# Modulation with eight and two column groups in one accumulator each, summed at the seams, and a gate's row sums by fp32r products

## The chip, the cores and the metric

One NeuronCore of a Trainium2 chip runs the whole kernel. The metric is the device time of one execution in microseconds. The kernel before takes 2351.67 us (median of three runs, 2350.42 to 2352.06).

## The reference, cut to what matters

Two transformer blocks of width 2048 over 256 tokens. The second block is modulated: a vector `c` of 2048 numbers goes through SiLU and through a weight matrix of 2048 by 12288, and the result, cut in six, shifts, scales and gates the two halves of the block:

```
c_act = jax.nn.silu(c)
mod = (c_act @ w_ada[l] + b_ada[l])[:, None, :]
sh1, sc1, g1, sh2, sc2, g2 = jnp.split(mod, 6, axis=-1)
h = rms_norm(x, norm_mix[l]) * (1.0 + sc1) + sh1
x = x + g1 * hybrid_mixer(h, ...)
h = rms_norm(x, norm_ffn[l]) * (1.0 + sc2) + sh2
x = x + g2 * conv_glu_ffn(h, ...)
```

All the rest (first block with attention, gated linear attention and a gated FFN; second block's mixer and FFN with a convolution) is unchanged by the change.

## The kernel before, in words

The kernel runs six stages one after the other: `FirstMixer`, `Glu`, `Down` (first FFN), `SecondMixer`, `ConvGlu`, `Down` again. Every large product is made in three fp32r products of high and low parts. Weights arrive from HBM over SP's DMA queue: `load` (L245 on) brings 1 MiB as two transfers of 512 KiB into a ring of four (`raw_weights`), ScalarE copies the high part (`split_hi`, L289), VectorE subtracts the low part (`split_lo`, L297), and TensorE multiplies (L330, L608, L1858, L2216). A unit is half a load; ScalarE and VectorE are three units ahead of TensorE. SP issues in program order, and each load waits until the ring's slot has been split.

The modulation (`c_act @ w_ada`, 96 MiB of weights) isn't done on TensorE. Its 12288 columns are cut in twelve groups of 1024 columns. `Ada.load` (L488 on) brings 256 rows of one group as one transfer of 1 MiB (128 partitions of two rows, 4 KiB each) into one of two buffers (`ada_w`); it waits until the products of the load before the last are done. `Ada.product` (L501 on) multiplies one of the two rows of each partition by its `c` on VectorE and adds it to an accumulator `ada_acc` of 128 partitions by 1024: sixteen steps a group, the first of which is a plain multiply (L518), the others multiply and add (L516). Then each group's accumulator has to be summed over its 128 partitions. The groups and what sums them:

- group 0: products in the last ticks of `FirstMixer`; groups 1 to 5: products in `Glu`, two turns each. Each of these six is summed in `Glu`: `turned` makes eight TensorE transposes (L460) and `reduced` one VectorE reduction of 128x1024 out of PSUM (L467).
- groups 6, 7, 8: products in `Down` (24 loads between k = 5 and the tail), each in an accumulator of its own. Groups 6 and 7 are summed at the start of `SecondMixer` with products by a column of ones (L1953, two instructions for each of the eight, since fp32 takes two), the last six of the second group's eight between `turn_early` (L2152) and the four `turn` (L2141) that the stage's first products wait for.
- group 8 goes to HBM and back, and group 9 (products in `SecondMixer`) too; both are summed at the start of `ConvGlu` (L3616 by ones, L460 by transposes), with the last columns' scales made inside the first turn (`last_scales`).
- groups 10 and 11, the second gate, are needed along the rows: `row_sums` (L3646) multiplies ones by the accumulator, in fp32, in two places of `ConvGlu`.

Of the kernel before, what the change touches and what calls it, by code (L numbers as in the profile page):

```python
# [21 lines left out]
ds = bass.ds  # L22
# [38 lines left out]

COLS = {}
_n = 0
for _name, _w in (("attn_norm_w", 16), ("ffn_norm_w", 16), ("norm_mix_2", 16), ("norm_ffn_2", 16), ("c_2", 16),
# [3 lines left out]
                  ("conv_w0", 88), ("conv_w1", 88), ("conv_w2", 88), ("conv_b", 88), ("b_ada_2", 96)):  # L68
# [13 lines left out]
def constants():  # L82
# [4 lines left out]
    parts = [("ident", r == c), ("ones", np.ones((P, P))), ("headsum", same),  # L87
             ("incl", same & (r <= c)), ("anti", same & (r >= c))]
# [33 lines left out]
class Kit:  # L122


    def __init__(self, nc, ctx, ins, at):
# [28 lines left out]
        self.ada_w = [self.sem("ada_w0"), self.sem("ada_w1")]  # L154
# [302 lines left out]
def turn_sums(kit, acc, bank):  # L457

    for q in range(8):
        step = kit.nc.tensor.transpose(kit.ps[:, bank + q // 4, (q % 4) * P:(q % 4 + 1) * P], acc[:, q * P:(q + 1) * P],  # L460
                                       kit.c("ident"))
    return step


def reduce_sums(kit, a, bank):

    return kit.nc.vector.tensor_reduce(kit.modcols[:, ds(a, 8)], kit.ps[:, bank:bank + 2, :].rearrange(  # L467
        "p b (q n) -> p (b q) n", n=P), AX, ALU.add)


def add_bias(kit, a, count):

    b = COLS["b_ada_2"] + a
    cols = kit.modcols[:, a:a + count]
    kit.dve(kit.nc.vector.tensor_tensor(cols, cols, kit.col[:, b:b + count], ALU.add))


class Ada:

    def __init__(self, kit, w, acc, free=None, stored=None):


        self.kit, self.w, self.acc, self.free, self.stored = kit, w, acc, free, stored

    def load(self, sp, lead, j, m):  # L488

        kit = self.kit  # L490
        if self.free:
            sp.wait_ge(*self.free)
            self.free = None
        a = 8 * lead + m
        if a >= 2:
            sp.wait_ge(kit.ada_acc, 2 * (a - 1) + 16 * j)
        w = kit.ins["w_ada_2"][0]
# [3 lines left out]
    def product(self, dve, lead, j, s, acc=None):  # L501
# [3 lines left out]
        if s == 0 and self.stored:  # L505
            dve.wait_ge(kit.ada_sum, lead - 1)
# [14 lines left out]
    def sums(self, pe, lead, j, bank=6):  # L521
# [3 lines left out]
        if lead > 1:  # L525
            pe.wait_ge(kit.ada_out, lead - 1 + j)
# [3409 lines left out]
```

## Time and profile before

| | |
|---|---|
| median of three runs | 2351.67 us |
| the profiled execution | 2352.51 us |
| its span, first to last instruction | 2350.7 us |
| granted clock of TensorE, mean | 0.997 |
| TensorE busy | 2337.8 us (99%) |
| TensorE weight loads busy | 2151.6 us (92%) |
| VectorE busy | 1616.4 us (69%) |
| ScalarE busy | 1153.2 us (49%) |
| SP's DMA queue, packets' time as a share of 16 engines | 68.3% |

"Busy" is the time in which at least one instruction of the engine was under way. [...] The share of a DMA queue is a mean over the 16 DMA engines; it says nothing on how the load is spread over them.

### The profile page before, as it was taken

What the parts mean: (1) busy time and instruction counts of PE and PEld (TensorE: products, weight loads), DVE (VectorE), ACT (ScalarE), POOL (GpSimd) and SP (SyncE); (2) the same over time, 40 slices, a digit from 0 to 9 for tenths busy, and PEclk for the clock granted to TensorE, in tenths of its full rate; (3) what the DMA queues carried; (4) which work ended last, traced back from release to release, by engine and by line L of the source; (5) the groups of instructions that cost most, each with busy time, mean ns of one, the idle gap of its engine ahead of it and who ended that gap; (6) DMA issues with size and microseconds to landing.
All of it is one profiled execution on the core that took longest, in us unless ns stands there. A gap on an engine that the chain in (4) does not pass through costs nothing.

```text
span 2350.7 us, 43754 instructions
## 1 busy us (share of the span) xinstructions
PE 2337.8 (99%) x17937; PEld 2151.6 (92%) x17937; DVE 1616.4 (69%) x1931; ACT 1153.2 (49%) x1510; POOL 5.1 (0%) x7
## 2 busy tenths in 40 slices
PE   9999999999999999999999999999999999999998
PEld 8889778999999999888999899888999999998887
DVE  5668568777777766877778455667878666665556
ACT  5565454534344344444764444546544445454444
POOL 0000000000000000000000000000000000000000
PEclk9999999999999999999999999999999999999999
DMA  8556567888888877898577545555778656665563
GB/s 308 167 179 197 159 234 271 278 282 297 282 282 295 282 242 263 316 324 315 175 279 269 163 130 153 196 200 187 283 255 295 208 179 206 196 206 197 192 192 117
DMA packets 233049, 543.62 MB, mean 231 GB/s; under 512 B 15610, under 2 KB 22596, under 8 KB 232260
## 3 DMA queue, kind: packets, MB, share of 16 engines
q1 hardware_dynamic: 232756, 540.97, 68.3%
q8 instruction: 110, 1.80, 0.3%
q10 hardware_dynamic: 144, 0.52, 0.1%
q14 instruction: 39, 0.32, 0.0%
HBM read 535.11 MB, written 6.32 MB: 230 GB/s over the span
## 4 chain that ended last, share of the span: by engine, by line
PE 98%; DVE 0%; ACT 0%; issue 0%; DMA 0%; SPq 0%; DVEq 0%; ACTq 0%
PE ps L330 37%; PE ps L1858 18%; PE ps L608 18%; PE ps L2216 16%; PE ps L1875 2%; PE ps L2509 0%; PE ps L1041 0%; PE ps L1053 0%; PE ps L1071 0%; PE ps L1083 0%; PE ps L2141 0%; PE ps L460 0%; PE ps L2744 0%; PE ps L1134 0%; PE ps L2921 0%
## 5 line engine op out<-in xcount | busy, mean ns | idle before, releaser
L297 DVE TENSOR_TENSOR weights_lo<-raw_weights,weights_hi 128x1024 fp32r<-128x1024 f32 x786 | 957.6, 1224 | 659.8 <-ACT weights_hi L289 658.0
L289 ACT ACTIVATE weights_hi<-raw_weights 128x1024 fp32r<-128x1024 f32 x782 | 827.2, 1062 | 1086.8 <-PE ps L330 446.4
L516 DVE SCALAR_TENSOR_TENSOR ada_acc<-ada_w,col,ada_acc 128x1024 f32<-128x1024 f32 x180 | 230.2, 1279 | 0.1
L330 PE MATMUL ps<-conv_x_hi,weights_hi 128*128 128x256 f32 x1280 | 198.0, 277 | 0.0
L330 PE MATMUL ps<-glu_x_hi,weights_hi 128*128 128x256 f32 x1280 | 197.7, 276 | 0.0
L330 PE MATMUL ps<-glu_x_hi,weights_lo 128*128 128x256 f32 x1280 | 197.2, 276 | 0.0
L330 PE MATMUL ps<-glu_x_lo,weights_hi 128*128 128x256 f32 x1280 | 197.2, 276 | 0.0
L330 PE MATMUL ps<-conv_x_lo,weights_hi 128*128 128x256 f32 x1280 | 197.2, 276 | 0.0
L330 PE MATMUL ps<-conv_x_hi,weights_lo 128*128 128x256 f32 x1280 | 197.2, 276 | 0.0
L330 PEld LDWEIGHTS ps<-conv_x_hi,weights_hi 128*128 128x128 f32 x1280 | 169.1, 188 | 1.0 <-issue 1.0
L330 PEld LDWEIGHTS ps<-glu_x_hi,weights_hi 128*128 128x128 f32 x1280 | 169.0, 188 | 0.0
L330 PEld LDWEIGHTS ps<-glu_x_lo,weights_hi 128*128 128x128 f32 x1280 | 168.9, 188 | 0.0
L330 PEld LDWEIGHTS ps<-glu_x_hi,weights_lo 128*128 128x128 f32 x1280 | 168.9, 188 | 0.0
L330 PEld LDWEIGHTS ps<-conv_x_hi,weights_lo 128*128 128x128 f32 x1280 | 168.9, 188 | 0.0
L330 PEld LDWEIGHTS ps<-conv_x_lo,weights_hi 128*128 128x128 f32 x1280 | 168.9, 188 | 0.0
L2216 PE MATMUL ps<-m_x_hi,weights_hi 128*128 128x256 f32 (+1 forms) x576 | 94.9, 288 | 0.1
L3800 DVE SCALAR_TENSOR_TENSOR conv_y<-ps,conv_taps,conv_y 128x255 f32<-128x255 f32 (+1 forms) x176 | 72.7, 476 | 29.8 <-ACT conv_y L3732 28.8
L2216 PE MATMUL ps<-m_x_lo,weights_hi 128*128 128x256 f32 (+1 forms) x576 | 89.8, 279 | 0.0
L2216 PE MATMUL ps<-m_x_hi,weights_lo 128*128 128x256 f32 (+1 forms) x576 | 89.2, 277 | 0.5 <-issue 0.5
L1858 PE MATMUL ps<-weights_hi,down_hi 128*128 128x512 f32 x288 | 89.0, 390 | 0.5 <-DVE stat L3804 0.2
L1858 PE MATMUL ps<-weights_hi,down_lo 128*128 128x512 f32 x288 | 88.7, 389 | 0.0
L1858 PE MATMUL ps<-weights_lo,down_hi 128*128 128x512 f32 x288 | 88.7, 389 | 0.0
(560 smaller groups left out, 3635.3 us busy)
## 6 DMA issues: line engine op xcount, KB each, us to landing
raw_weights<-in_w_in_dram SPq DMA_DIRECT2D x202, 512.0 KB, 5.0
ada_w<-in_w_ada_dram SPq DMA_DIRECT2D x96, 1024.0 KB, 6.1
raw_weights<-in_w_ffn_up_dram SPq DMA_DIRECT2D x176, 512.0 KB, 4.6
raw_weights<-in_w_gate_dram SPq DMA_DIRECT2D x88, 512.0 KB, 4.6
raw_weights<-in_w_up_dram SPq DMA_DIRECT2D x88, 512.0 KB, 4.6
raw_weights<-in_w_down_dram SPq DMA_DIRECT2D x88, 512.0 KB, 5.7
raw_weights<-in_w_ffn_down_dram SPq DMA_DIRECT2D x88, 512.0 KB, 4.3
raw_weights<-in_w_out_dram SPq DMA_DIRECT2D x64, 512.0 KB, 5.1
```

Of the source, the lines that this page charges most:

```text
L289: kit.nc.scalar.activation(kit.slots(n, i)[0], raw, ACT.Copy).then_inc(kit.w_hi, 1)
L297: kit.nc.vector.tensor_tensor(lo, raw, hi.bitcast(F32), ALU.subtract).then_inc(kit.w_lo, 1)
L330: ins = nc.tensor.matmul(out, lhsT=lhsT, rhs=rhs, start=start and m == 0, stop=(k == KT - 1 and m == 2), skip_group_check=True)
L516: step = nc.vector.scalar_tensor_tensor(acc, w, c, acc, ALU.mult, ALU.add)
L608: ins = nc.tensor.matmul(out, lhsT=lhsT, rhs=rhs, start=start and m == 0, stop=ends and m == 2, skip_group_check=True)
L1858: ins = nc.tensor.matmul(kit.ps[:, 4 * t + 2 * half + q, :], lhsT=lhsT, rhs=rhs, start=(k == 0 and m == 0), stop=ends and m == 2, skip_gro ...
L1875: ins = nc.tensor.matmul(kit.ps[:, 4 * t + 2 * half + q, :], lhsT=lhsT, rhs=w[:, q * UN:(q + 1) * UN], start=False, stop=k == w_tiles - 1 ...
L2216: ins = nc.tensor.matmul(out, lhsT=lhsT, rhs=rhs, start=start and m == 0, stop=ends and m == 2, skip_group_check=True)
L3800: nc.vector.scalar_tensor_tensor(y[:, j, q, b:S], self.tile(j, q)[:, 0:S - b], taps[:, j, tap, q:q + 1], y[:, j, q, b:S], ALU.mult, ALU.ad ...
```

## The change

The partition dimension of the accumulators is cut up. For the first eight groups (columns 0 to 8191) the 128 partitions hold eight groups of sixteen rows: step `s` takes sixteen rows of the matrix, and partition 16 g + r holds row r of group g. After 128 such steps one accumulator holds the eight groups, sixteen partitions each, and eight products with a mask of 128 by 8 (`oct`) sum all of them at the start of `SecondMixer`. Groups 8 and 9 are held in one accumulator in the same way, two groups of 64 rows (mask `half`, 32 steps), and are summed at the start of `ConvGlu`. Groups 10 and 11 are loaded as before. The number of steps (192) and of bytes stays. The sums of `Glu` (transposes and reductions) go; the accumulator is carried over from stage to stage (`prior`), only the second pair's goes through HBM, once. `c` is needed in two more layouts (`c_half`, `c_oct`), the latter by one more pack, its transpose and a small copy each two turns of `Glu`. Each load is now two transfers of 512 KiB, whose source is `(g n)` columns taken as `g r n`. The gate's accumulator is split in a high part (ScalarE) and a low part (VectorE), and its row sums are four fp32r products in place of two fp32 ones.

```diff
 class Ada:
+    def source(self, lead, j, s):
+
+        w = self.kit.ins["w_ada_2"][0]
+        if lead < 8:
+            rows = w[ds(OCT * (16 * lead + s) + 16 * OCT * j, OCT), 0:16 * UN]
+        elif lead < 10:
+            rows = w[HALF * (16 * (lead - 8) + s):HALF * (16 * (lead - 8) + s + 1), 16 * UN:20 * UN]
+        else:
+            rows = w[P * s:P * (s + 1), 2 * UN * lead:2 * UN * (lead + 1)]
+        return rows.rearrange("r (g n) -> g r n", n=2 * UN)
 
     def load(self, sp, lead, j, m):
...
-        sp.dma_start(self.w[:, m % 2, :, :], w[2 * m * P:2 * (m + 1) * P, ds(2 * UN * lead + 2 * UN * j, 2 * UN)]
-                     .rearrange("(k p) n -> p k n", p=P)).then_inc(kit.ada_w[m % 2], 16)
+        for s in (2 * m, 2 * m + 1):
+            sp.dma_start(self.w[:, m % 2, s % 2, :], self.source(lead, j, s)).then_inc(kit.ada_w[m % 2], 16)
...
+    def sums(self, pe, bank, mask, acc):
+
+        kit, (a, b) = self.kit, self.kit.at[mask]
+        n = b - a
         for q in range(8):
-            step = nc.tensor.matmul(kit.ps[:, bank, q:q + 1], lhsT=self.acc[:, q * P:(q + 1) * P],
-                                    rhs=kit.c("ones")[:, 0:1], start=True, stop=True)
+            step = kit.nc.tensor.matmul(kit.ps[:, bank, n * q:n * (q + 1)], lhsT=acc[:, q * P:(q + 1) * P],
+                                        rhs=kit.c(mask), start=True, stop=True)
         step.then_inc(kit.ada_sum, 1)
...
+    def summed(self, lead, bank, mask):
+
+        kit, (a, b) = self.kit, self.kit.at[mask]
+        n, first, bias = b - a, 8 * lead, COLS["b_ada_2"] + 8 * lead
+        cols, add = (x.rearrange("p (g q) -> p q g", q=8) for x in (kit.modcols[:, first:first + 8 * n],
+                                                                    kit.col[:, bias:bias + 8 * n]))
+        return kit.nc.vector.tensor_tensor(cols, kit.ps[:, bank, 0:8 * n].rearrange("p (q g) -> p q g", g=n), add, ALU.add)
...
 class Glu:
...
-            mid = (lambda: self.ada.turned(pe, self.lead, j)) if summed else None
...
-                if summed and s == begun:
-                    self.ada.reduced(dve, self.lead, j)
                 if half is not None and s % 2 == begun:
-                    self.ada.product(dve, self.lead, j, 8 * half + s // 2)
+                    q = 8 * half + s // 2
+                    if q == 0:
+                        a = COLS["c_oct"] + 16 * self.lead
+                        dve.wait_ge(kit.ada_acc, 16 * self.lead + 16 * j)
+                        nc.vector.tensor_copy(self.c_turn[:, :], kit.col[:, ds(a + 16 * j, 16)]).then_inc(self.s_c, 1)
+                        dve.wait_ge(self.s_c, 1 + j)
+                    self.ada.product(dve, self.lead, j, q, c=self.c_turn[:, q:q + 1])
...
 class SecondMixer:
...
     def tensor(self, pe):
         kit, nc = self.kit, self.kit.nc
         pe.wait_ge(self.squares_in, 8)
-        self.down.ada_sums(pe, 0)
-        self.down.ada_sums(pe, 1, 0, 2)
+        self.down.ada_sums(pe)
         pe.wait_ge(self.squares_in, 11)
         for k in range(4):
             self.turned.turn_early(pe, k)
-        self.down.ada_sums(pe, 1, 2, 8)
         for k in range(4):
             self.turned.turn(pe, k)
...
 class ConvGlu:
...
+    def scales(self, dve):
+
+        dve.wait_ge(self.kit.ada_sum, 2)
+        self.kit.dve(self.ada.summed(8, 1, "half"))
+
+    def row_sums(self, pe, g):
+
+        kit, nc = self.kit, self.kit.nc
+        pe.wait_ge(self.s_acclo, g + 1)
+        for b in range(2):
+            for acc in (self.acc_hi, self.acc_lo):
+                step = nc.tensor.matmul(kit.ps[:, 4 + 2 * g + b, :], lhsT=self.ones[:, :], rhs=acc[:, b * UN:(b + 1) * UN],
+                                        start=acc is self.acc_hi, stop=acc is self.acc_lo)
         step.then_inc(kit.ada_sum, 1)
```

## Rows read from the trace of the kernel before

**Rows 1.** The page: busy time of the engines; the chain that ended last, by engine.

```profile
PE 2337.8 (99%) x17937; PEld 2151.6 (92%) x17937; DVE 1616.4 (69%) x1931; ACT 1153.2 (49%) x1510; POOL 5.1 (0%) x7
...
PE 98%; DVE 0%; ACT 0%; issue 0%; DMA 0%; SPq 0%; DVEq 0%; ACTq 0%
```

**Rows 2.** Timeline of Glu's last sum (start, us, engine, line, operation, count).

```profile
866.08 1.04 PE L460 MATMUL ps<-cst,ada_acc 128*128 128x128 f32 x8
...
866.87 0.72 PE L330 MATMUL ps<-glu_x_hi,weights_hi 128*128 128x256 f32 x4
867.21 1.22 DVE L467 TENSOR_REDUCE modcols<-ps 128x8 f32<-128x1024 f32 x1
```

**Rows 3.** Timeline of the second gate's first row sums, and of 512-column products.

```profile
1131.26 0.62 PE L1875 MATMUL ps<-down_last_hi,glu_x_hi 128*128 128x512 f32 x2
...
1131.72 0.61 PE L1875 MATMUL ps<-down_last_lo,glu_x_hi 128*128 128x512 f32 x2
...
1731.30 0.62 PE L330 MATMUL ps<-conv_x_hi,weights_lo 128*128 128x256 f32 x4
...
1731.75 1.88 PE L3646 MATMUL ps<-ada_acc,cst 128*128 128x512 f32 x4
...
1733.94 0.64 PE L330 MATMUL ps<-conv_x_lo,weights_hi 128*128 128x256 f32 x4
```

**Rows 4.** Timeline of the start of the second mixer.

```profile
1150.20 2.25 PE L1953 MATMUL ps<-cst,ada_acc 128*128 128x1 f32 x12
...
1150.21 0.17 DVE L3547 SCALAR_TENSOR_TENSOR modT<-modcols,col 128x16 f32<-128x16 f32 x1
...
1150.44 0.71 ACT L2117 ACTIVATE m_scaled<-x_weighted,stat 128x512 f32<-128x512 f32 x1
...
1152.32 1.09 PE L2141 MATMUL ps<-cst,m_scaled 128*128 128x128 f32 x4
```

**Rows 5.** Windows (us; busy of each engine; PEclk, DMA share, GB/s): the two seams.

```profile
1151.00:1152.00 1.00, 1.00 (x6) 1.00 (x6) 0.84 (x3) 0.14 (x1) 0.00 (x0) 0.50 1.24 256
...
1158.00:1160.00 2.00, 2.00 (x20) 2.00 (x19) 1.21 (x3) 1.46 (x4) 0.00 (x0) 1.00 0.78 207
...
1616.00:1617.00 1.00, 0.67 (x6) 0.46 (x6) 0.57 (x2) 1.00 (x3) 0.00 (x0) 1.00 0.99 389
```

**Rows 6.** Windows: the four stretches in which modulation weights of groups 0 to 9 arrive.

```profile
325.70:421.00 95.30, 95.14 (x439) 78.43 (x439) 74.59 (x82) 50.08 (x70) 0.00 (x0) 1.00 0.86 309
...
478.30:856.00 377.70, 377.70 (x3334) 377.70 (x3333) 280.75 (x236) 154.95 (x147) 0.00 (x0) 1.00 0.83 288
...
913.00:1110.00 197.00, 197.00 (x871) 163.13 (x870) 153.40 (x155) 87.58 (x109) 0.00 (x0) 1.00 0.89 321
...
1191.00:1265.00 74.00, 74.00 (x611) 72.08 (x610) 62.57 (x71) 41.41 (x56) 0.00 (x0) 1.00 0.85 313
```

**Rows 7.** DMA view of 320 to 420 us: GB/s in forty slices of 2.5 us.

```profile
GB/s 0 202 283 415 403 395 404 388 386 388 392 375 401 189 209 367 374 292 41 293 336 406 209 180 374 370 316 98 376 329 61 0 167 401 406 385 370 191 355 411
```

**Rows 8.** Timeline of SP: modulation loads in Glu, in Down, and first and last in the second mixer.

```profile
481.78 0.48 SPq L498 DMA_DIRECT2D ada_w<-in_w_ada_dram  x1
...
492.66 0.47 SPq L498 DMA_DIRECT2D ada_w<-in_w_ada_dram  x1
...
1004.50 0.38 SPq L498 DMA_DIRECT2D ada_w<-in_w_ada_dram  x1
...
1012.66 0.38 SPq L498 DMA_DIRECT2D ada_w<-in_w_ada_dram  x1
...
1191.11 0.37 SPq L498 DMA_DIRECT2D ada_w<-in_w_ada_dram  x1
...
1256.26 0.37 SPq L498 DMA_DIRECT2D ada_w<-in_w_ada_dram  x1
```

**Rows 9.** Timeline of SP: issues of vectors of 16 rows and of 4 rows.

```profile
16.17 0.42 SPq L829 DMA_DIRECT2D pack<-in_c_dram  x1
...
17.39 0.29 SPq L829 DMA_DIRECT2D pack<-in_rwkv_w_dram  x1
```

More of the change, by code:

```diff
@@ L503, in product, with scalar @@
+    def scalar(self, lead, s):
+        name, first = ("c_oct", 0) if lead < 8 else ("c_half", 8) if lead < 10 else ("c_2", lead)
+        return self.kit.cols(name, 16 * (lead - first) + s)
+    def product(self, dve, lead, j, s, acc=None, prior=None, c=None):
         nc, kit = self.kit.nc, self.kit
         m, k = s // 2, s % 2
-        if s == 0 and self.stored:
-            dve.wait_ge(kit.ada_sum, lead - 1)
-            dve.wait_ge(self.stored, 16)
-        elif s == 0 and lead and acc is None:
-            dve.wait_ge(kit.ada_sum, lead + j)
@@ L827, in sync @@
         for n in range(1, len(self.packs)):
-            for at, to, width, src in self.packs[n][0]:
-                sp.dma_start(self.pack[at:to, n, 0:width], src).then_inc(self.s_packs, 16)
+            tile = self.c_rows if n == len(self.packs) - 1 else self.pack[:, n, :]
+            for at, to, lo, hi, src in self.packs[n][0]:
+                sp.dma_start(tile[at:to, lo:hi], src).then_inc(self.s_packs, 16)
         bias = self.mem["bias_dram"].ap()
@@ L944, in turn_pack @@
         _, w, _ = self.packs[n]
-        kit.nc.tensor.transpose(kit.ps[:, 6, 0:w], self.pack[0:w, n, :], kit.c("ident")[0:w, 0:w]
-                                ).then_inc(self.s_packT, 1)
+        last = n == len(self.packs) - 1
+        if last:
+            pe.wait_ge(self.s_cwide, 1)
+        rows = self.pack[0:w, 0 if last else n, :]
+        kit.nc.tensor.transpose(kit.ps[:, 6, 0:w], rows, kit.c("ident")[0:w, 0:w]).then_inc(self.s_packT, 1)
     def spread_scale(self, at):
@@ L1330, in pack_out @@
         _, w, at = self.packs[n]
+        if n == len(self.packs) - 2:
+            dve.wait_ge(self.s_packs, 16 * sum(len(p[0]) for p in self.packs[1:]))
+            self.kit.nc.vector.tensor_copy(self.pack[:, 0, :].rearrange("p (g r) -> p g r", r=OCT),
+                                           self.c_rows[:, :].unsqueeze(1).broadcast_to([P, P // OCT, OCT])
+                                           ).then_inc(self.s_cwide, 1)
         dve.wait_ge(self.s_packT, n + 1)
@@ L1809, in sync @@
         kit, first, w_tiles = self.kit, self.first, self.w_tiles
[L1810 to L1812 removed]
+        loads = 8 * self.joint
         def due(k):
@@ L3610, in scale_sums @@
     def scale_sums(self, pe):
-        kit, mixer = self.kit, self.mixer
-        pe.wait_ge(mixer.s_accs, 16)
-        pe.wait_ge(kit.pair_free[0], self.uses[0] + 1)
-        for q in range(8):
-            step = kit.nc.tensor.matmul(kit.ps[:, 1, q:q + 1], lhsT=mixer.accs[:, 0, q * P:(q + 1) * P],
-                                        rhs=kit.c("ones")[:, 0:1], start=True, stop=True)
-        step.then_inc(kit.ada_sum, 1)
-        pe.wait_ge(mixer.s_xlast, ST)
-        turn_sums(kit, mixer.accs[:, 1, :], 2).then_inc(kit.ada_sum, 1)
@@ L3648, in row_sums, with acc_split @@
         step.then_inc(kit.ada_sum, 1)
+    def acc_split(self, i, j, u, after):
+        g, off = divmod(16 * i + 8 * j + u - 36 - after, self.GROUP) if isinstance(i, int) else (0, 1)
+        return g if off == 0 and 0 <= g < 2 else None
     def sync(self, sp):
```

233 lines of the change are left out of this document (96 added, 137 removed).

## The prediction

> **What bounds the kernel now.** I read the page first. TensorE is busy 99% of the span, and the chain that ended last runs over TensorE for 98% of it [rows 1]. The reader is to see that nothing else is late: VectorE and ScalarE have room, and what TensorE doesn't have to do comes off the end one for one, as long as its weights are there in time. Then I read the timeline at each place where the change takes TensorE work away [rows 2 to 4] and the granted clock at the two seams [rows 5]. Last, since the change rewrites the source of 80 MiB of loads, I read the windows over the stretches in which these loads arrive [rows 6], the rate of the DMA view [rows 7] and the spacing of the loads [rows 8]. That last reading decides the forecast. In all four stretches the DMA engines are busy between 83 and 89% of the time [rows 6]: the kernel is bound by TensorE with only some 11 to 17% between it and a second bound.
>
> **What the change takes from TensorE.** Six sums in Glu, eight transposes each. From the start of the transposes to the start of the next product it is 0.79 us, and the eight of them last 1.04 us [rows 2]; I take 0.9 us a sum, 5.4 us in all. The second gate's row sums: from their start to the second group of products behind them it is 1733.94 - 1731.75 = 2.19 us, of which one group of four products is 1731.75 - 1731.30 = 0.45, so the sums cost 1.74 us. In their place come four fp32r products of 512 columns; two of these take 1131.72 - 1131.26 = 0.46 us, so four take 0.92 [rows 3]. That saves 0.8 us at each of two places, 1.6 us. At the start of the second mixer the transposes L2141 begin at 1152.32, behind twelve products by ones that began at 1150.20, while the scaled tile was ready at 1150.44 + 0.71 = 1151.15 [rows 4]. Without the twelve they can begin 1.17 us earlier. VectorE now forms all 64 columns (`ada_summed`) ahead of `modulation` in this chain, one more small operation of 0.17 us as L3547 [rows 4] and a wait for itself: 0.3 us. What is late next is the scaled tile. Gain 0.9 us. At the seam to ConvGlu the sums lie in a wait for the last norm, so they give nothing, and one wait more on VectorE costs 0.1 us. One more pack's transpose and its wait cost 0.1 us. Sum: 5.4 + 1.6 + 0.9 - 0.2 = 7.7 us off.
>
> **What I cost at nothing.** VectorE loses seven reductions of 1.22 us [rows 2]. It gains two subtractions of the same size for the gate's low part, and ScalarE two copies; both lie two to three units ahead of the row sums that wait for them. If that cover were gone, TensorE would wait at most for one of each, some 2.5 us at each of two places, with the unit's own products queued behind. In Glu a copy of sixteen columns and two waits come before each turn pair's first product, with `split_lo` queued behind on VectorE; it is idle 97 of 378 us there [rows 6]. The last norm's weight is loaded later in Down, but long before its use. SP issues 80 more transfers at about 0.4 to 0.5 us each [rows 8]; between two loads it has 8 us and more.
>
> **The loads: the term that decides.** Until now every large transfer has 128 as its outermost count on both sides (`(k p) n -> p k n`). In the change the source of groups 0 to 7 is `r (g n) -> g r n` with eight g outermost, and that of groups 8 and 9 has two g outermost. The rows of 4 KiB and the bytes are the same. The question is over how many of the sixteen DMA engines such a transfer is spread. No large transfer of this kind is in the trace. The nearest rows are the small vectors: SP takes 0.42 us to issue one of sixteen rows and 0.29 us for one of four rows [rows 9], so the work of an issue follows the row count, as it would if the transfer were dealt out by its outermost count. That leans to eight engines for the first kind and two for the second; it doesn't prove it.
>
> [...]
>
> The price of it. Where the DMA engines have a backlog they deliver about 400 GB/s (slices of 383 to 415 [rows 7]), so 1 MiB costs 1.0486 MB / 400 GB/s = 2.62 us of all sixteen, 5.24 us on eight and 21 us on two. All transfers go through one queue in order, and a weight load has landed only when its part on the slowest engine has. So the loaded engines set the pace. The upper bound of each term uses the busy share of the rows, which is higher than bytes over rate: share times spacing over the MiB in it, 2.9 to 3.0 us per MiB.
> - First mixer, eight loads in 95.3 us. 309 GB/s are 28 MiB, 73 us by rate; with 21 us more it is 94, just inside. By share 82 + 23 = 105, 10 over [rows 6]. I take +2 (0 to 10).
> - Glu, 40 loads, one each 492.66 - 481.78 = 10.9 us [rows 8] with 2 MiB of weights. By rate 3 x 2.62 + 2.62 = 10.5 us, just inside. By share 0.83 x 10.9 = 9.0, plus 3.0 = 12.0: 1.2 us over, 47 in all [rows 6]. I take +5 (-5 to 47), near the rate's end, since rows 7 show that rate sustained. The 5.4 us of transposes are spent here, since TensorE no longer has any slack of its own to give: the +5 is net of them.
> - Down, groups 6 and 7, sixteen loads each 1012.66 - 1004.50 = 8.16 us with 1.5 MiB of weights. By rate 2.5 x 2.62 + 2.62 = 9.2: 1.0 over, 16 in all; by share 7.3 + 2.9 = 10.2, 32 in all. I take +16.
> - Down, group 8, eight loads on two engines: 1.5 x 2.62 + 21 = 24.9 us each in place of 8.16, +134 (by share +155; less up to 20 for what the ring holds ahead at the beginning).
> - Second mixer, group 9, eight loads between 1191 and 1265 [rows 8]: 313 GB/s over 74 us [rows 6] are 22 MiB, 14 of them others, 37 us; plus 8 x 21 = 168 is 205 us in place of 74, +131. Some of the others can wait till after, so I take +125 (105 to 149).
>
> Sum: 2 + 5 + 16 + 134 + 125 = 282, less what is still gained outside these stretches, 1.6 + 0.9 - 0.2 = 2.3: +280. On the profiled execution's 2352.5 us that is 2632; the median lies 0.8 below it, and the forecast for the median is 2631. Low end of this case: 0 - 5 + 10 + 114 + 105 - 3 = +221, 2573. High end: 10 + 47 + 32 + 155 + 149 = +393, 2745. [...]
>
> **The rivals.** (1) The split goes by the 128 partitions of the destination, or by bytes, and all sixteen engines work as before. Then only the 7.7 us off stay: 2344.0. For it: the bytes, the rows of 4 KiB and the destination are unchanged, and rows 9 are small. Against it: they are the only rows that tell issues of different shape apart, and they differ. (2) As (1), but the clock falls at the seam to ConvGlu too, where eight transposes less fill the wait. In the kernel before it stayed at 1.00 there with TensorE busy only 0.67 us of one [rows 5], and fell at the other seam. Some seven microseconds at half, as there, of which half is lost: +3.5, so 2347.5. It decides from the point where the fillers are gone; the sign stays. (3) Eight engines but also a common limit below them, so that Glu too runs at the share's price: the high end of the forecast's case, 2745. The forecast is on the slower side, and (1) is the rival on the other side, one mechanism at one place: the outermost count doesn't steer the spread.
>
> **How the numbers follow.** Few engines, with the forecast 2631: 0.84 (of it rival 3: 0.08). Rival 1: 0.13. Rival 2: 0.03. What a measurement of this kernel can tell from no change is about 0.2%, 4.7 us: rival 1 is faster by 0.33%, rival 2 by 0.18%. So faster 0.13, same 0.03, slower 0.84. The range leaves out rivals 1 and 2, 0.16, and takes the whole of the forecast's case with some room at both ends for the absorption and the share: 2550 to 2785.
>
> **What would show it.** Right: a modulation load of groups 8 and 9 lands some 20 us after its issue or more, in Down and in the second mixer; TensorE waits for weights there, and idles with low clock; in these stretches the mean DMA share falls to about a quarter to a third though the queue is never empty, since two engines of sixteen are busy; Glu's turn (four loads, 43.6 us) stays or grows by at most 10%. The savings are seen all the same: no L460 in Glu, row sums of 0.9 us, L2141 a microsecond nearer to the last product of Down. Wrong: modulation loads land in 6 us as before and the DMA share stays at 0.8 to 0.9 (rival 1); or Down grows but the second mixer doesn't, which would say that the ring and the products' order hide more than I allow.

## The result, and the profile after

The change makes the kernel slower: 2821.88 us (median of four runs, 2812.13 to 2832.97) against 2351.82 before (median of four), a ratio of 1.200 (95% interval 1.195 to 1.205). That is +470 us, where the forecast had +280 and a range up to 2785. The profiled execution took 2817.98 us, its span is 2816.2.

The page of the kernel after: busy time; granted clock and GB/s in 40 slices; the chain that ended last, by engine and by line (compare [rows 1]).

```profile
PE 2439.0 (87%) x17866; PEld 2225.7 (79%) x17866; DVE 1601.8 (57%) x1929; ACT 1152.5 (41%) x1514; POOL 5.1 (0%) x7
...
PEclk9999999999999899886779767999999999999999
...
GB/s 290 174 187 163 157 247 254 227 224 225 223 222 222 214 196 230 223 181 100 102 132 191 105 88 172 163 156 119 217 195 291 249 266 194 189 183 220 194 193 128
...
PE 53%; DMA 31%; DVE 8%; SPq 5%; issue 2%; ACT 0%; DVEq 0%; ACTq 0%
DMA ada_w<-in_w_ada_dram 29%; PE ps L335 18%; PE ps L2204 11%; PE ps L580 10%; PE ps L1857 8%; DVE weights_lo L302 4%; DMA raw_weights<-in_w_in_dram 2%; SPq L258 2%; SPq L487 2%; DVE ada_acc L506 1%; PE ps L1874 1%; DVE ada_acc_oct L506 1%;
```

TensorE bounded the kernel for 98% of the chain; now it is 53%, and the modulation's transfers hold 29%. To see where, I read the time at which SP issues the first modulation load of Glu, of Down, of Down's group 8, of the second mixer and of ConvGlu. Timeline of SP, kernel before (the first of the second mixer is in [rows 8], 1191.11), then after:

```profile
413.89 0.47 SPq L498 DMA_DIRECT2D ada_w<-in_w_ada_dram  x1
...
913.20 0.43 SPq L498 DMA_DIRECT2D ada_w<-in_w_ada_dram  x1
...
1045.30 0.38 SPq L498 DMA_DIRECT2D ada_w<-in_w_ada_dram  x1
...
1612.17 0.37 SPq L498 DMA_DIRECT2D ada_w<-in_w_ada_dram  x1
```

```profile
431.44 1.92 SPq L487 DMA_DIRECT2D ada_w<-in_w_ada_dram  x1
...
1053.38 0.67 SPq L487 DMA_DIRECT2D ada_w<-in_w_ada_dram  x1
...
1245.29 6.33 SPq L487 DMA_DIRECT2D ada_w<-in_w_ada_dram  x2
...
1532.39 4.54 SPq L487 DMA_DIRECT2D ada_w<-in_w_ada_dram  x2
...
2078.50 0.82 SPq L487 DMA_DIRECT2D ada_w<-in_w_ada_dram  x2
```

The differences of these times, stretch by stretch, beside the forecast's terms:

| stretch | before | after | more | forecast |
|---|---|---|---|---|
| up to Glu's first load (group 0) | 413.9 | 431.4 | +17.5 | +2 |
| Glu (groups 1 to 5) and Down's head | 499.3 | 622.0 | +122.7 | +5 |
| Down, groups 6 and 7 | 132.1 | 191.9 | +59.8 | +16 |
| Down, group 8, to the second mixer's first load | 145.8 | 287.1 | +141.3 | +134 |
| second mixer (group 9) | 421.1 | 546.1 | +125.0 | +125 |
| the rest | 738.5 | 737.7 | -0.8 | -2.3 |

The loads on two engines cost what was forecast, 266 against 259. Those on eight cost 200 against 23. Windows of the first four stretches and of the first 208 us of the fifth, kernel after (columns as in [rows 5]; compare [rows 6]):

```profile
324.20:431.40 107.20, 98.44 (x431) 79.52 (x430) 70.02 (x78) 44.93 (x60) 0.00 (x0) 0.95 0.87 241
431.40:1053.40 622.00, 533.56 (x4280) 524.66 (x4279) 352.56 (x317) 211.38 (x217) 0.00 (x0) 0.93 0.74 223
1053.40:1245.30 191.90, 154.88 (x607) 123.48 (x606) 100.88 (x104) 60.83 (x76) 0.10 (x1) 0.89 0.78 222
1245.30:1532.40 287.10, 158.88 (x766) 133.43 (x765) 112.39 (x149) 83.33 (x127) 0.00 (x0) 0.77 0.39 125
1532.40:1740.00 207.60, 110.13 (x735) 105.10 (x733) 69.85 (x76) 44.54 (x60) 0.00 (x0) 0.76 0.37 113
```

In Glu the share fell from 0.83 to 0.74 although the queue holds the kernel up. That fits eight engines: per load eight of them carry 2/16 + 1/8 = 0.25 MiB, the others 0.125; if the eight are never idle and all packets take the same time, the mean share is (1 + 0.5) / 2 = 0.75. In Down's second part and the second mixer it is 0.39 and 0.37, and while the loads of group 8 come 25 us apart it is 0.32:

```profile
1268.00:1422.20 154.20, 63.81 (x216) 49.74 (x216) 37.80 (x39) 21.48 (x27) 0.00 (x0) 0.70 0.32 104
```

The share is a mean, and other things can move it. The traces have a count that is nearer to the question: how many times the DMA engines raised the two semaphores that tell of the landing of modulation loads. In plain16 and quad (below), with 128, 32 or 64 outermost entries, it is 3072 for 192 transfers, sixteen each. In the kernel after it is 1760, which is 128 x 9 + 32 x 3 + 32 x 16, for the 128 transfers of groups 0 to 7, the 32 of groups 8 and 9 and the 32 of groups 10 and 11. So a transfer of eight entries leaves nine marks and one of two entries three, in place of sixteen: as many as entries, and one more. With 64 entries for groups 8 and 9 (half_rg below) it is 2176, which is 128 x 9 + 64 x 16. And in short stretches the share stands at a plain fraction of sixteen engines: 0.51 from 600 to 604.5 us in Glu, eight of them, and 0.13 at 53 GB/s from 1284 to 1291 us, among group 8's loads, two of them. The weight loads among group 8's show it too: fourteen of the sixteen marks of one land from 1341.15 to 1342.12 us, the last two at 1354.77 and 1359.04. I read all this together as eight and two engines.

How a late load reaches TensorE is seen at group 8's first step. Timeline, kernel after (idle time and its releaser in brackets):

```profile
1269.66 11.13 SPq L487 DMA_DIRECT2D ada_w<-in_w_ada_dram  x1
1279.54 0.75 DVE L503 TENSOR_SCALAR ada_acc_half<-ada_w,col 128x1024 f32<-128x1024 f32 x1 [18.86 <-DMA ada_w<-in_w_ada_dram]
1280.21 1.22 DVE L302 TENSOR_TENSOR weights_lo<-raw_weights,weights_hi 128x1024 fp32r<-128x1024 f32 x1
1280.79 1.06 ACT L294 ACTIVATE weights_hi<-raw_weights 128x1024 fp32r<-128x1024 f32 x1 [18.28 <-DMA raw_weights<-in_w_down_dram]
...
1281.58 1.19 PE L1857 MATMUL ps<-weights_hi,glu_x_hi 128*128 128x512 f32 x2 [14.78 <-DVE weights_lo L302]
...
1283.42 1.05 PE L1857 MATMUL ps<-weights_hi,glu_x_lo 128*128 128x512 f32 x2
...
1284.27 1.05 PE L1857 MATMUL ps<-weights_hi,glu_x_hi 128*128 128x512 f32 x2
...
1289.32 0.61 PE L1857 MATMUL ps<-weights_hi,glu_x_lo 128*128 128x512 f32 x2
...
1289.77 0.62 PE L1857 MATMUL ps<-weights_hi,glu_x_hi 128*128 128x512 f32 x2
```

VectorE stands 18.86 us before the modulation's product, `split_lo` is queued behind it, and TensorE waits 14.78 us for that. ScalarE waits 18.28 us for the weight load on the same queue: a late transfer reaches TensorE by two ways. Afterwards two products take 1284.27 - 1283.42 = 0.85 us from start to start of the next two, later 1289.77 - 1289.32 = 0.45. The granted clock goes with it: 0.50 behind the stall, and 1.00 again from 1288 on. Windows, kernel after:

```profile
1284.00:1286.00 2.00, 2.00 (x7) 1.52 (x6) 1.23 (x2) 0.00 (x0) 0.00 (x0) 0.50 0.13 53
...
1288.00:1290.00 2.00, 2.00 (x11) 1.63 (x9) 0.00 (x0) 0.49 (x2) 0.00 (x0) 1.00 0.13 53
```

The waits of the kernel after (us in total, times, longest) say the same of the whole:

```profile
DVE ada_acc L506 <- DMA ada_w<-in_w_ada_dram: 389.9, 52, 21.1
...
ACT weights_hi L294 <- DMA raw_weights<-in_w_down_dram: 154.0, 14, 20.8
...
DVE ada_acc_half L506 <- DMA ada_w<-in_w_ada_dram: 136.3, 7, 21.7
...
DVE ada_acc_oct L506 <- DMA ada_w<-in_w_ada_dram: 92.2, 16, 9.3
```

### The profile page after: what moved, and what is told of

It is laid out like the page before. It is cut to its first block, busy times and chain, and to the rows that moved or that the text cites. A ratio compares the mean times of both kernels' runs of the same rounds, so it can differ in the third digit from the quotient of the medians.

```text
span 2816.2 us, 43779 instructions
## 1 busy us (share of the span) xinstructions
PE 2439.0 (87%) x17866; PEld 2225.7 (79%) x17866; DVE 1601.8 (57%) x1929; ACT 1152.5 (41%) x1514; POOL 5.1 (0%) x7
## 4 chain that ended last, share of the span: by engine, by line
PE 53%; DMA 31%; DVE 8%; SPq 5%; issue 2%; ACT 0%; DVEq 0%; ACTq 0%
DMA ada_w<-in_w_ada_dram 29%; PE ps L335 18%; PE ps L2204 11%; PE ps L580 10%; PE ps L1857 8%; DVE weights_lo L302 4%; DMA raw_weights<-in_w_in_dram 2%; SPq L258 2%; SPq L487 2%; DVE ada_acc L506 1%; PE ps L1874 1%; DVE ada_acc_oct L506 1%; PE ps L2491 0%; DVE ada_acc_half L506 0%; SPq L809 0%
## 5 line engine op out<-in xcount | busy, mean ns | idle before, releaser
L335 PE MATMUL ps<-glu_x_hi,weights_hi 128*128 128x256 f32 x1280 | 215.6, 293 | 84.1 <-DVE weights_lo L302 84.0
L335 PEld LDWEIGHTS ps<-glu_x_hi,weights_hi 128*128 128x128 f32 x1280 | 183.3, 202 | 90.5 <-DVE weights_lo L302 89.2
L506 DVE SCALAR_TENSOR_TENSOR ada_acc<-ada_w,glu_c,ada_acc 128x1024 f32<-128x1024 f32 x80 | 102.5, 1282 | 247.9 <-DMA ada_w<-in_w_ada_dram 243.9
L335 PE MATMUL ps<-glu_x_lo,weights_hi 128*128 128x256 f32 x1280 | 208.6, 287 | 0.0
L335 PEld LDWEIGHTS ps<-glu_x_lo,weights_hi 128*128 128x128 f32 x1280 | 180.8, 200 | 0.0
L506 DVE SCALAR_TENSOR_TENSOR ada_acc<-ada_w,col,ada_acc 128x1024 f32<-128x1024 f32 x60 | 76.8, 1280 | 134.7 <-DMA ada_w<-in_w_ada_dram 134.6
L1857 PE MATMUL ps<-weights_hi,glu_x_hi 128*128 128x512 f32 x192 | 68.0, 438 | 97.6 <-DVE weights_lo L302 97.5
L2204 PEld LDWEIGHTS ps<-m_x_hi,weights_hi 128*128 128x128 f32 (+1 forms) x576 | 84.9, 204 | 68.7 <-DVE weights_lo L302 66.0
L1857 PEld LDWEIGHTS ps<-weights_hi,glu_x_hi 128*128 128x128 f32 x192 | 39.7, 214 | 110.6 <-issue 102.7
L1857 PEld LDWEIGHTS ps<-weights_hi,down_hi 128*128 128x128 f32 x288 | 57.4, 203 | 81.2 <-issue 68.4
```

What stands on the lines that cost most here:

```text
L335: ins = nc.tensor.matmul(out, lhsT=lhsT, rhs=rhs, start=start and m == 0, stop=(k == KT - 1 and m == 2), skip_group_check=True)
L506: step = nc.vector.scalar_tensor_tensor(acc, w, c, acc if prior is None else prior, ALU.mult, ALU.add)
L1857: ins = nc.tensor.matmul(kit.ps[:, 4 * t + 2 * half + q, :], lhsT=lhsT, rhs=rhs, start=(k == 0 and m == 0), stop=ends and m == 2, skip_gro ...
L2204: ins = nc.tensor.matmul(out, lhsT=lhsT, rhs=rhs, start=start and m == 0, stop=ends and m == 2, skip_group_check=True)
```

## The experiments

The theory to begin with: few engines, by the outermost count of the source. The rival: the loads are slow for their addresses, or the sums cost something. Then, why the loads on eight engines cost so much more than forecast.

**plain16**: all modulation loads from 128 plain rows of one group; the rest is the change's.

```diff
-            rows = w[ds(OCT * (16 * lead + s) + 16 * OCT * j, OCT), 0:16 * UN]
...
+        rows = w[P * s:P * (s + 1), ds(2 * UN * lead + 2 * UN * j, 2 * UN)]
```

> The changed kernel with one thing taken back: every modulation transfer reads 128 rows of one group of 1024 columns, so that 128 is outermost on both sides, as before. It reads other numbers than the change needs, so the modulation's sums and the output are not the reference's. All else of the change stays: 192 transfers of 512 KiB, masks, no sums in Glu, fp32r row sums. Theory A (the whole loss is in how the transfers are spread and written): 2344 us, that is the 7.7 us less that TensorE has to do, ratio 0.9967. Rival (something else of the change also costs, such as the doubled number of transfers, the waits, or a lower clock at a seam): above 2352 us.

Measured 2345.51 us, ratio 0.9975 (0.9965 to 0.9984). The whole loss is in the form of the loads; the sums at the seams, masks and splits give a gain.

**half_two**: groups 8 and 9 as two transfers of 64 partitions, one for each group.

```diff
+                for g in range(2):
+                    src = kit.ins["w_ada_2"][0][at:at + HALF, (8 + g) * 2 * UN:(9 + g) * 2 * UN]
+                    sp.dma_start(self.w[g * HALF:(g + 1) * HALF, m % 2, s % 2, :], src).then_inc(kit.ada_w[m % 2], 16)
```

> The changed kernel with groups 8 and 9 loaded by two transfers of 64 partitions for each one of 128, the same bytes to the same places, each with 64 outermost on both sides in place of 2. Theory A (the outermost count sets the number of engines): the loads that now come each 25 us in Down and each 24.8 us in the second mixer come each 8 to 9 us again, 138 + 124 = 262 us less: 2560 us. Modulation loads of groups 0 to 7 stay at 14.1 us apart in Glu and 12.0 us in Down. Rival (the two engines are not what makes them late; smaller transfers don't help): 2822 us, or more for the added issues.

Measured 2585.79 us, ratio 1.103 (1.097 to 1.109): two engines account for 2822 - 2586 = 236 us, and 240 stay over plain16. As in the table above, most of what was mis-sized lies in groups 0 to 7. It is 26 us more than expected; half_rg below says why.

**apart8** cuts each load of groups 0 to 7 in four transfers of 32 partitions, still eight outermost entries; **rows8** reads plain rows as eight blocks of sixteen, the destination as in the change. Both with half_two's edit.

```diff
+                for q in range(4):
+                    src = w[ds(OCT * (16 * lead + s) + 4 * q + 16 * OCT * j, 4), 0:16 * UN].rearrange(
+                        "r (g n) -> g r n", n=2 * UN)
+                    sp.dma_start(self.w[32 * q:32 * (q + 1), m % 2, s % 2, :], src).then_inc(kit.ada_w[m % 2], 16)
...
+            rows = w[120 * s:120 * s + 136, ds(2 * UN * lead + 2 * UN * j, 2 * UN)]
+            return rows.rearrange("(e r) n -> e r n", r=17)[:, 0:16, :]
```

> As half_two, and each 128-partition transfer of groups 0 to 7 is cut in four of 32 partitions with eight groups outermost and four rows inside. [...] Theory S (it is the source: eight engines read eight neighbouring pieces of the same matrix row at once): the source pattern is the same, so still 14.1 and 12.0 us and 2560 us. Theory E (eight engines carry twice the load and that alone makes it so): 2560 us too.

> As half_two, but groups 0 to 7 are read from plain rows of one column group: eight blocks of sixteen rows, seventeen rows from block to block, so that eight stays the outermost count and the destination (sixteen neighbouring partitions for each of eight engines) stays as in the change. The numbers read are not those the change needs, so the output is not the reference's. Theory W (write path): as half_two, 2560 us, loads 14.1 us apart in Glu. Theory S (source pattern): the eight engines no longer read neighbouring pieces, so 10.9 to 11.5 us apart and about 2390 us.

Measured apart8 2502.22 us, ratio 1.064 (1.058 to 1.070); rows8 2571.07, ratio 1.093. What is read hardly matters: rows8 has half_two's 14.1 us in Glu and ends within 1% of it. How the transfer is cut does (12.9 us in apart8), but apart8 came out 58 us under the 2560 of theories S and E, and it changes the destination and the number of transfers together. It also shows that the share over a whole stretch doesn't prove the number of engines by itself: it has eight outermost entries too (nine marks a transfer; 6144 in all, 512 x 9 + 96 x 16), and its share in Glu is 0.84.

**inter16**: the complete result with the row outermost, so sixteen entries.

```diff
-        return rows.rearrange("r (g n) -> g r n", n=2 * UN)
+            return rows.rearrange("r (g n) -> r g n", n=2 * UN)
...
+             ("oct", r % 8 == np.arange(P // OCT)[None, :])
```

> Groups 0 to 7 keep the change's rows of 4 KiB and its sums at the seams, but the source is taken as r g n with the sixteen rows r outermost, so that destination partition 8r+g holds row r of group g; the mask follows (partition modulo eight), and c is repeated eight times in a row instead of the block of sixteen being repeated. Groups 8 and 9 are two transfers of 64 partitions. The result is complete. Theory (the outermost count of either side sets the engines, and sixteen engines with eight partitions each are the pattern of the kernel before): Glu's loads come 10.9 us apart and Down's 8.2, as in plain16, and the time is that of plain16, 2345 to 2348 us, ratio 0.997 to 0.9985: faster than both kernels. Rival (a source that jumps from one group's columns to the next costs something by itself, at sixteen engines too): loads of 12 us in Glu and over 9 in Down, 2390 us or more.

Measured 2436.53 us, ratio 1.037 (1.034 to 1.040). My theory fell: sixteen marks a transfer (3584 for 224) and a share of 0.95 in Glu, so sixteen engines, and still 91 us over plain16. By the same stretches as above, 70 of these are in Glu and in groups 6 and 7 (533.1 us against plain16's 493.5, 162.1 against 132.3); 24 are behind them, where groups 8 and 9 come by half_two's edit.

**far16, near16, same16**: the same form, sixteen entries of eight, with other addresses. In far16 entry e is rows e, e + 16, e + 32 and on of one column group, so entries lie one row apart, as in inter16, and none walks along a row. In near16 entry e is row 8e over the eight column groups, so entries lie eight rows apart and each walks along a row in steps of 4 KiB, as in inter16. In same16 entry e is rows 9e to 9e + 7 of one column group, nearly what plain16 reads. All three read other weights than the reference, and their output is another one.

```diff
+            rows = w[P * s:P * (s + 1), ds(2 * UN * lead + 2 * UN * j, 2 * UN)]
+            return rows.rearrange("(i e) n -> e i n", e=16)
...
+            rows = w[P * s:P * (s + 1), 0:16 * UN]
+            return rows.rearrange("(e i) (g n) -> e i g n", i=8, n=2 * UN)[:, 0]
...
+            rows = w[120 * s:120 * s + 144, ds(2 * UN * lead + 2 * UN * j, 2 * UN)]
+            return rows.rearrange("(e i) n -> e i n", i=9)[:, 0:8, :]
```

> [...] Theory 1 (the distance of one row between engines is what slows inter16): Glu's loads 12.4 us apart, near 2436 us. Theory 2 (it is the walk along a row of 32 KiB in steps of 4 KiB): Glu's loads 10.9 us apart, near 2346 us.

> [...] The modulation comes from other weights and the output is another one. Theory 1 (distance of one row between engines): Glu's loads 10.9 us apart, near 2346 us. Theory 2 (walk along a row): 12.4 us apart, near 2436 us.

> [...] The modulation comes from other weights and the output is another one. Theory A (addresses: the orders of inter16, far16 and near16 are bad ones and the plain one is good): Glu's loads 10.9 us apart, near 2346 us. Theory B (form: with sixteen outermost entries of eight rows each the sixteen engines' packets are dealt and written in another order than with 128 entries, whatever they read): 12.4 us apart, near 2435 us.

Measured 2429.12, 2439.8 and 2447.46 us (ratios 1.033, 1.038, 1.041). far16 and near16 were to tell two addresses apart and both were slow, which neither theory had; same16 settled it. It isn't the addresses, it is the form.

**pair8**: as apart8 in eight transfers of 16 partitions, to see where apart8's gain over half_two, 84 us, came from.

```diff
-                for q in range(4):
+                for q in range(8):
...
+                    sp.dma_start(self.w[16 * q:16 * (q + 1), m % 2, s % 2, :], src).then_inc(kit.ada_w[m % 2], 16)
```

> [...] Theory C (the gain came from cutting the transfer into pieces): Glu's loads 12.9 us apart or less, 2500 us or less.

Measured 2699.26 us, and it tells nothing of its question. Timeline of SP, pair8:

```profile
725.28 14.17 SPq L497 DMA_DIRECT2D ada_w<-in_w_ada_dram  x16
...
742.21 14.58 SPq L497 DMA_DIRECT2D ada_w<-in_w_ada_dram  x16
```

Sixteen issues take SP 14.17 us, so a load takes 742.21 - 725.28 = 16.9 us of it: the kernel was bound by issuing, with a DMA share of 0.57 in Glu (460 to 840 us).

**join2, join4**: 64 entries of two rows and 32 entries of four, row outermost, with half_two's edit. The diff is join4's; join2 has `P // 2` and `4 * UN`.

```diff
+            rows = w[P * s:P * s + P // 4, 0:8 * UN]
+            return rows.rearrange("r (g n) -> r g n", n=2 * UN)
```

> Groups 0 to 7 read 64 rows by two column groups with the row outermost, so 64 outermost entries of two rows of 4 KiB; groups 8 and 9 as in half_two. The modulation comes from other weights and the output is another one. Theory B (the order in which the outermost entries are dealt to sixteen engines): four entries for each engine, an order between that of plain16 and that of inter16, Glu's loads between 10.9 and 11.5 us, 2346 to 2380 us. Theory A (addresses): two column groups side by side walk along a row as near16 does; near 2435 us if that is bad, 2346 if not.

> As join2 with 32 rows by four column groups: 32 outermost entries of four rows of 4 KiB, two for each engine. Theory B: more than join2 and at most inter16, 2360 to 2436 us. If join2 and join4 both stand at 2346, only the last step, one outermost entry for each engine, is bad.

Measured 2354.83 (2346.65 to 2362.25) and 2355.3 us (2348.97 to 2364.55). In Glu and in groups 6 and 7 the loads come as in plain16, 10.9 and 8.2 us apart. So 32 entries are good in this stretch and sixteen of eight partitions are bad. join4 came under the 2360 us that its theory B had at the least: the spacing doesn't grow little by little from 128 entries to sixteen. Both medians lie some 10 us over plain16, and that is half_two's edit: join4's groups 0 to 7 come as in plain16, but from group 8's first load to the second mixer's first it takes 152.1 us against 145.1. Against join4, which has the same edit, the sixteen entries of inter16 cost 81 us.

**side4**: inter16's load in two transfers, each sixteen entries of four column pieces and so four partitions.

```diff
+                for q in range(2):
+                    src = w[ds(OCT * (16 * lead + s) + 16 * OCT * j, OCT), 8 * UN * q:8 * UN * (q + 1)].rearrange(
+                        "r (g n) -> r g n", n=2 * UN)
+                    sp.dma_start(self.w[64 * q:64 * (q + 1), m % 2, s % 2, :], src).then_inc(kit.ada_w[m % 2], 16)
```

> As inter16 with the complete result, but each load of groups 0 to 7 is two transfers of 64 partitions, sixteen rows by four column groups with the row outermost: one outermost entry for each of sixteen engines as in inter16, but four rows and four partitions in it as in join4. Theory N (one entry for each engine is what is slow): Glu's loads 12 us apart or more, 2430 us or more. Theory E (an entry of eight rows is what is slow): Glu's loads near 10.9 us apart, 2350 to 2365 us.

Measured 2370.08 us, ratio 1.008 (1.006 to 1.010), 10.9 us apart in Glu. So mostly the size of the entry, though it is 5 us over the theory's range. Its packets are still slow; windows of 460 to 840 us (Glu) of same16, side4 and quad (below), one each:

```profile
460.00:840.00 380.00, 357.03 (x3074) 353.34 (x3073) 250.07 (x219) 141.98 (x136) 0.00 (x0) 0.99 0.94 264
```

```profile
460.00:840.00 380.00, 380.00 (x3355) 380.00 (x3354) 284.25 (x241) 156.50 (x148) 0.00 (x0) 1.00 0.96 289
```

```profile
460.00:840.00 380.00, 380.00 (x3355) 380.00 (x3354) 285.13 (x241) 155.75 (x149) 0.00 (x0) 1.00 0.86 290
```

quad and side4 move the same bytes, 290 and 289 GB/s, with shares of 0.86 and 0.96. GB/s over share is 337 and 301; in same16 it is 264 / 0.94 = 281. The share is the packets' time over that of 16 engines, and it passes 1 in places (1.04 in join4's window below, 1.24 in [rows 5]). So I take the quotient as an estimate of how fast packets go, not as a rate that was seen. The same reading of the other kernels in this window:

| kernel | outermost entries | share, GB/s | GB/s over share | us between Glu's loads |
|---|---|---|---|---|
| before | 128 | 0.83, 287 | 346 | 11.0 |
| plain16 | 128 | 0.84, 290 | 345 | 10.9 |
| join4 | 32 of 4 | 0.85, 290 | 341 | 10.9 |
| side4 | 2 x 16 of 4 | 0.96, 289 | 301 | 10.9 |
| inter16 | 16 of 8 | 0.95, 265 | 279 | 12.0 |
| near16 | 16 of 8 | 0.97, 266 | 274 | 12.0 |
| after | 8 of 16 | 0.75, 227 | 303 | 14.1 |
| half_two | 8 of 16 | 0.76, 226 | 297 | 14.1 |
| apart8 | 4 x 8 of 4 | 0.84, 246 | 293 | 12.9 |

With eight or sixteen partitions in an entry the quotient is 274 to 303 against 341 to 346 with 128 entries or 32 of four, and Glu's loads come 12.0 to 14.1 us apart against 10.9 to 11.0: the queue holds the kernel up. For side4's 301 there are two candidates: sixteen outermost entries of four partitions, or two transfers of 64 partitions in place of one of 128. No run has the first without the second. The second alone is in join4's groups 8 and 9, 64 entries of one partition in each transfer, beside quad's one transfer of 64 entries of two. Windows of the first 72.6 us of the second mixer, join4 and quad:

```profile
1191.80:1264.40 72.60, 71.36 (x592) 69.61 (x590) 60.39 (x66) 41.32 (x56) 0.00 (x0) 1.00 1.04 287
```

```profile
1188.40:1261.00 72.60, 72.60 (x599) 70.69 (x599) 61.73 (x68) 41.36 (x56) 0.00 (x0) 1.00 0.85 309
```

GB/s over share is 276 in join4 and 364 in quad. So in join4 transfers of 64 partitions have slow packets with 64 outermost entries too, and nothing shows that sixteen entries add to it.

**rows_only**: the second part of the change, the fp32r row sums, in the kernel before.

```diff
-            step = nc.tensor.matmul(kit.ps[:, 4 + 2 * g + b, :], lhsT=kit.c("ones"),
-                                    rhs=self.ada.acc[:, b * UN:(b + 1) * UN], start=True, stop=True)
+            for acc in (self.acc_hi, self.acc_lo):
+                step = nc.tensor.matmul(kit.ps[:, 4 + 2 * g + b, :], lhsT=self.ones[:, :], rhs=acc[:, b * UN:(b + 1) * UN],
+                                        start=acc is self.acc_hi, stop=acc is self.acc_lo)
```

> One part of the change alone, made in the kernel before: the second gate's row sums as fp32r products of a high and a low part. Complete result. The prediction's term for it is 0.8 us at each of two places, 1.6 in all: 2351.8 - 1.6 = 2350.2 us, ratio 0.9993. Rival (the split for the low part comes late on VectorE, and TensorE waits at both places for about 1 us): 2352 us, ratio 1.0.

Measured 2350.66 us, ratio 0.9994 (0.9985 to 1.0003); from ConvGlu's first modulation load to the end of the span it is 737.0 us against 738.5, -1.5 for two places.

**half_rg**: the change with groups 8 and 9 read with the row outermost, in one transfer.

```diff
-        return rows.rearrange("r (g n) -> g r n", n=2 * UN)
+        return rows.rearrange("r (g n) -> g r n" if lead < 8 or lead > 9 else "r (g n) -> r g n", n=2 * UN)
```

> The change with one edit: groups 8 and 9 are read with the row outermost (64 entries of two rows of 4 KiB) in the same single transfer, so on sixteen engines; the destination's halves then mix rows and groups, and the modulation of these two groups is another one. Groups 0 to 7 stay on eight engines. If groups 8 and 9 as two transfers of 64 partitions cost half_two 10 us: 2576 us. If they cost nothing: 2586 us as half_two.

Measured 2561.87 us, ratio 1.089. Two engines thus cost 2822 - 2562 = 260 us; the forecast had 259 for them. half_two's two transfers cost some 24 us of their own beside loads on eight engines (two runs and four, so the 24 is rough), more than the 10 that I had expected and that they cost in join2 and join4.

**quad**: the complete result with 32 and 64 entries. The even column groups of the first eight go to one accumulator, the odd ones to a second.

```diff
-            rows = w[ds(OCT * (16 * lead + s) + 16 * OCT * j, OCT), 0:16 * UN]
+            rows = w[ds(QUAD * (8 * lead + s // 2) + 8 * QUAD * j, QUAD), 0:16 * UN]
+            return rows.rearrange("r (g k n) -> k r g n", k=2, n=2 * UN)[s % 2]
...
+        acc = (self.acc2 if k and lead < 8 else self.acc) if acc is None else acc
```

> A complete version of the change with another layout. Groups 0 to 7: each transfer takes 32 rows by four column groups with the row outermost (32 entries of four rows of 4 KiB), the even groups into one accumulator, the odd ones into a second; masks are the partition modulo four; at the second mixer's start sixteen small products in place of eight. Groups 8 and 9: one transfer of 64 entries of two. Theory (only the outermost count of the loads was wrong, and 32 or 64 entries are as good as 128): loads as in plain16 (10.9 us apart in Glu, 8.16 in Down), plain16's 2345.5 plus 1 us for eight products more at the second mixer's start: 2346 to 2348 us, ratio 0.998, faster than both kernels. Rival (join2's and join4's 10 us over plain16 belong to 32 and 64 entries and not to the two transfers of groups 8 and 9): 2355 us or more, ratio 1.0013.

Measured 2348.03 us (2346.67 to 2350.03, 11 runs), ratio 0.9982 (0.9973 to 0.9991): less than 0.2% faster than the kernel before, though clear of no change by its interval, where the change as it stands was 20% slower. Timeline of SP, quad:

```profile
416.61 0.54 SPq L488 DMA_DIRECT2D ada_w<-in_w_ada_dram  x1
...
910.09 1.23 SPq L488 DMA_DIRECT2D ada_w<-in_w_ada_dram  x2
...
1188.40 1.20 SPq L488 DMA_DIRECT2D ada_w<-in_w_ada_dram  x2
...
1609.44 0.82 SPq L488 DMA_DIRECT2D ada_w<-in_w_ada_dram  x2
```

Glu's stretch is 910.09 - 416.61 = 493.5 us against 499.3 before.

## Why the prediction was right or wrong

**The mechanism was right, but not all of it.** Ahead of the result only the issues of [rows 9] leaned to a spread by the outermost count. The traces show it for the change's counts of eight and two: plain16 takes the loss away whole, the marks are nine and three a transfer in place of sixteen, and the share stands at 0.51 and 0.13 in short stretches and is 0.74 to 0.75 over Glu. The rivals 1 and 2 fell. What the mechanism left out is that the form of a transfer can also make its packets slower, with sixteen marks a transfer too (inter16: 279 GB/s over share against plain16's 345).

**Two engines: right in size.** Group 8's eight loads are issued from 1245.29 to 1422.2, 25.3 us apart against 24.9; with group 9 the terms were 134 + 125 and came out at 141.3 + 125.0. The price of 400 GB/s for sixteen engines holds here: 1.5 + 8 = 9.5 MiB of sixteen engines' work in 25.3 us is 2.66 us per MiB, against 2.62. That holds for the two engines that set the pace. By the same price the mean share would be 0.26, an estimate from these terms; it is 0.32, so by this estimate packets on the other fourteen took longer. That cost nothing there: fourteen marks of each weight load among group 8's come 4.8 us or more before its last two.

**Eight engines: the step that failed** is Glu's term, "By rate 3 x 2.62 + 2.62 = 10.5 us, just inside" and "I take +5 (-5 to 47), near the rate's end", with the same price in the first mixer (+2, measured +17.5) and in groups 6 and 7 (+16, measured +59.8). Glu's loads came 14.1 us apart and the stretch took 122.7 us more; the prediction's own sign, a turn of 43.6 us that grows by at most 10%, was missed by far (4 x 14.1 = 56.4). That is four MiB of sixteen engines' work (2 + 2 x 1) at 3.5 us each; in Down it is 3.5 MiB in 12.0 us, 3.4 each. Two things may lie on each other:
- The 400 GB/s of [rows 7] hold there for ten slices in a row at most, 25 us, and not "sustained"; by the share the engines of the kernel before move 346 GB/s in Glu, 3.0 us per MiB. At that price, the upper bound of the forecast, it is 12.0 us, 1.2 over, 47 us in Glu. I had this number and chose the other, where forty loads in a row would have had to run at it without a gap. Whether it was the better price isn't shown: no run fills the queue in Glu with loads of the old form, and at the seam [rows 5] they move 389 GB/s at a share of 0.99.
- The form itself is a cost that no row of before bounded, since none had a transfer with so few entries of so many partitions; from 12.0 to 14.1 us it is the only candidate that a run shows. The experiments show it on sixteen engines too, where no engine is missing: 2436.5 us for inter16 against 2355.3 for join4, with Glu's loads 12.0 us apart at a share of 0.95. Of the 216 us that groups 0 to 7 cost (half_rg 2561.9 less plain16 2345.5), I can't say how much belongs to the doubled load of eight engines and how much to slow packets; that stays open.

Rival 3, with the dearer price of the two, was the better choice, and at 2745 it was still 77 us short for the second reason. The range ended at 2785 because it allowed for nothing that the rows didn't show.

**The savings of TensorE: 7.7 forecast, 7.1 in plain16's profiled span (2350.7 - 2343.6), 5.6 between medians.** Glu's six sums: its stretch in plain16 is 493.5 us in place of 499.3, -5.8 against 5.4. The row sums: from 1726.19 to 1727.12 is 0.93 us against 0.92 forecast, timeline of plain16:

```profile
1726.19 0.40 PE L3605 MATMUL ps<-ada_acc_hi,ones_rounded 128*128 128x512 f32 x1
...
1727.12 0.64 PE L335 MATMUL ps<-conv_x_hi,weights_hi 128*128 128x256 f32 x4
```

rows_only gives -1.5 for both places (1.6 forecast). The second mixer's start, timelines of plain16 and, below it, of the kernel before:

```profile
1142.56 1.84 PE L509 MATMUL ps<-cst,ada_acc_oct 128*128 128x8 f32 x16
...
1146.40 1.09 PE L2124 MATMUL ps<-cst,m_scaled 128*128 128x128 f32 x4 [1.48 <-DVE m_scaled L2113]
```

```profile
1147.59 2.29 PE L1953 MATMUL ps<-cst,ada_acc 128*128 128x1 f32 x20
```

From the first sum to the transposes it is 3.84 us; before it was 1152.32 [rows 4] less 1147.59, 4.73. So 0.89 against 0.9, and the scaled tile is what is late next, as forecast: TensorE stands 1.48 us for it.

**Rival 2's clock did come, beside all else.** At the seam to ConvGlu the clock stayed at 1.00 before [rows 5] and is 0.50 in the kernel after (2083 to 2085 us) and in plain16, whose windows are:

```profile
1610.00:1611.00 1.00, 0.94 (x5) 0.57 (x4) 0.43 (x2) 0.95 (x3) 0.00 (x0) 0.50 0.98 375
1611.00:1612.00 1.00, 1.00 (x6) 1.00 (x6) 0.96 (x3) 1.00 (x4) 0.00 (x0) 0.50 0.54 209
```

ConvGlu is 0.9 us shorter in plain16 and 1.5 in rows_only, which keeps the transposes there and stays at 1.00; by these two traces the fall so costs about 0.6 us, not 3.5. The 3% were for the fall with sixteen engines, against 13% without it; eight transposes less in a gap with TensorE at 0.67 deserved the larger part.

## What to carry to other kernels

When a source is cut in another order, look at its outermost count first. Here, with rows of 4 KiB into 128 partitions, two entries cost 260 us over sixteen loads of 1 MiB; eight and sixteen entries cost 216 and some 70 to 80 us over 64 loads, and 32, 64 or 128 entries nothing. Of these counts the last three are the ones to take where a kernel leans on its loads. Keep all 128 partitions in one transfer: two of 64 cost join4 7 us in Down. Where the slack beside a stretch is a tenth of it, price the loads by GB/s over share in that stretch and not by the best slices (here 346 and not 400 GB/s, which gives 12.0 us of the 14.1), and reach the range beyond it if the form of the transfer has no row. And a late transfer costs more than its engine's idle time where an in-order engine has the next stage's work queued behind the wait: VectorE stood 18.86 us for the modulation, which had time, and `split_lo`, which had none, stood behind it, so that TensorE waited 14.78 us.

## What the runs showed that I had not expected

- With sixteen outermost entries of eight partitions GB/s over share is 274 to 281 in Glu, whatever the addresses (inter16 279, far16 281, near16 274, same16 281), where it is 337 to 346 with 128 or 32. In transfers of 64 partitions with 64 entries each it is as low (join4, second mixer, 276). Why wasn't shown: the traces name no engine and no partition of a packet, apart8 changed two things together, and pair8 couldn't be read.
- An issue behind late transfers keeps SP: the one at 1269.66 lasted 11.13 us where one takes 0.38 [rows 8]; what kept it wasn't shown. And sixteen small ones take 14.17 us in pair8, 0.9 each, where the larger ones of the kernel before take 0.47 to 0.48 in Glu [rows 8].
- Two transfers of 64 partitions are dearer than one of 128 of the same bytes: the second mixer takes 427.4 us in half_two and 420.5 in half_rg. In join4 it is 421.9, with 7 us more in Down.
